# A two-layer hybrid diffusion kernel: 18 modulation chunks computed as running sums within layer 0's gates, and the x stores of layer 1 on ScalarE's queue

## The chip, the cores and the metric

One Trainium2 chip, one of its cores. The time is the device time of one execution in microseconds (us), and less is better. All data is fp32; the large products run as three fp32r matmuls over split operands.

## What is computed

Two layers over 1024 latent tokens and 256 context tokens of width 1024. In each layer a modulated RMS norm is followed by an input projection, whose columns feed three token mixers (2-D Fourier mixing, neighbourhood attention, a short gated convolution); their results are projected, gated and merged, projected again and added to x; then follows a mixture of 16 experts. What the change touches is the modulation. It comes from two condition vectors, one for the latent tokens and one for the context:

```
for l in range(DEPTH):                       # DEPTH = 2, d = 1024
    mod   = silu(c)     @ ada_w[l] + ada_b[l]   # ada_w[l]: 1024 x 6144
    mod_c = silu(c_ctx) @ ada_w[l] + ada_b[l]
    sh1, sc1, g1, sh2, sc2, g2 = split(mod, 6)  # shift, scale, gate of both halves
```

`ada_w` of both layers is 24 chunks of 512 columns, 2 MB each. For one chunk and one vector w the result is the sum over 1024 rows: 8 groups of rows (k), 128 partitions in each.

## The kernel before

The kernel is a list of stages, seven per layer (`arrive_and_project`, `conv_branch`, `fourier_branch`, `attention`, `gates_and_merge`, `mix_and_route`, `experts`) and a closing one. Each stage is a block with a program for every engine: TensorE (`pe`), ScalarE (`act`), VectorE (`dve`), GpSimd (`pool`) and SyncE (`sp`), which issues nearly all DMAs. All engines meet at the end of a stage. The order within an engine is that of the code, and the engines are held together by semaphores: `wait_ge` waits until one has a value, `then_inc` raises it when an instruction is done.

**The modulation** (class `Modulations`, lines 238 to 302). Of the 24 chunks 4 are computed at the start of layer 0. The other 20 are spread over two stages of layer 0: 16 in `conv_branch` (one after roughly every product, `ada_at`, line 861) and 4 in `fourier_branch` (`modulations`, lines 1013 and 1080). For each chunk SP loads 2 MB (line 259). `multiply` (line 273) runs 8 matmuls with the two condition columns as the stationary operand and 512 columns of weights moving, four of them side by side on strips of the array; each fp32 matmul shows as two records. VectorE copies four pairs of rows out of PSUM (line 282). After the next product `turn` (line 290) runs 4 matmuls with a 128×128 stationary operand and 2 moving columns, which transpose the rows and add the four strips. VectorE adds the bias and keeps the columns (line 298).

**The convolution** (`conv_branch`, line 840). Six work items of three products each (two halves of the channels; token spans of 512, 512 and 256), 24 fp32r matmuls per product (lines 217 to 219). VectorE multiplies, and at the end of each half runs the convolution. SP loads the cosines of the next stage when chunk 14 is multiplied (line 875).

**The Fourier stage** (`fourier_branch`, line 965). Products over the tokens with cosines and sines (line 1021), then over the channels (lines 1041 to 1057). On SP's queue stand the first chunk's load, the sines, three small tables, the other three chunk loads, each waiting for the product before it, and then the first loads of attention's q, k and bias.

**The gates** (`gates_and_merge`, line 1504). A loop over 8 groups of 128 output channels (i and b), in each over three branches (q) and three token spans of 512, 512 and 256. For each span TensorE computes the gate (24 fp32r matmuls) and the branch's projection (2, 4 and 2 fp32 matmuls for the three branches, line 1577); ScalarE takes the sigmoid (line 1595), VectorE multiplies (line 1621), and GpSimd adds branches 1 and 2 to the sum (line 1643). At a branch's first span ScalarE and VectorE round and split the next branch's gate weights (lines 1586 and 1605). SP loads the weights of the next group when a branch is through (line 1500). Three pairs of PSUM banks turn round, so TensorE may be two spans ahead of VectorE; banks 6 and 7 are free. GpSimd first clears a tile of zeros (line 1630), with which SP fills the accumulator in HBM when the last gate weights are issued.

**The start of layer 1** (`arrive_and_project`, line 326, with `layer` 1). SP loads the experts' sums for ten token tiles (line 439), the context's x, a table and weights. For each tile VectorE updates x (`update`, lines 687 and 691), ScalarE squares it (`measure`, line 585), VectorE scales and shifts (lines 699 and 707), TensorE transposes (line 485), and ScalarE (`copy_turned`, line 595) writes the rounded transposed rows over the place of x. So it waits until x is stored in HBM, by SP (line 448). SP's loop alternates between the stores of x and those of v:

```
            for t in range(NT + 2):
                if layer and t < NT:
                    sp.wait_ge(s_up, t + 1)
                    sp.dma_start(s["x_rows"][t * P:(t + 1) * P], X[:, t]).then_inc(s_xst[t % 4], 16)
                if t >= 2:
                    sp.wait_ge(s_vc, t - 1)
```

Of the kernel before, what the change touches and what calls it, by code (L numbers as in the profile page):

```python
# [231 lines left out]
def apart(eng, passed):  # L232


    eng.sem_inc(passed, 1)  # L235
# [69 lines left out]
CONV_CHUNKS = 16  # L305
FOURIER_CHUNKS = 2 * Modulations.CH - FIRST_CHUNKS - CONV_CHUNKS

# [18 lines left out]
def arrive_and_project(s, layer, last):  # L326
# [77 lines left out]
    with nc.Block() as block:  # L404
        @block.sync
        def _(sp):
# [157 lines left out]
        def _(act):  # L564
# [275 lines left out]
def conv_branch(s, layer, last):  # L840
# [16 lines left out]
    if layer == 0:  # L857
# [3 lines left out]
        ada_at = {i * 3 * len(work) // CONV_CHUNKS: i for i in range(CONV_CHUNKS)}  # L861
# [103 lines left out]
def fourier_branch(s, layer, last):  # L965
# [9 lines left out]
    ada_weights = [place(at, KD, 512)]  # L975
# [13 lines left out]
    modulate = layer == 0  # L989
    if modulate:  # L990
        ada = Modulations(s, FIRST_CHUNKS + CONV_CHUNKS, FOURIER_CHUNKS, ada_weights, place(A_ATT + 4096, 512))
    with nc.Block() as block:
        @block.sync
        def _(sp):
            s["clear_last"](sp)
            consts = s["a"]["consts"]
            if modulate:
                ada.load(sp, 0)
# [13 lines left out]
        def _(pe):  # L1012
            def modulations(i):
                if modulate and 0 < i <= FOURIER_CHUNKS:
                    ada.turn(pe, i - 1)
                if modulate and i < FOURIER_CHUNKS:
                    ada.multiply(pe, i)

# [6 lines left out]
            for w in range(2):  # L1025
                if w:
                    pe.wait_ge(s_c, 16)
                for ct in range(2):
                    over_tokens(2 * w + ct, H, ct, range(NTX), lambda m: cb[w][:, m, :])
                    modulations(2 * w + ct)  # L1030
# [12 lines left out]
            modulations(4)  # L1043
# [3 lines left out]
            if not last:  # L1047
                for w in range(2):
                    for ct in range(2):
                        over_tokens(2 * w + ct, CTX, ct, range(NTX, NT), lambda m: dctx[:, m, w, :])  # L1050
                        modulations(5 + 2 * w + ct)
# [27 lines left out]
        def _(dve):  # L1079
            def modulations(i):  # L1080
                if modulate and i:
                    ada.keep(dve, i - 1)
                if modulate and i < FOURIER_CHUNKS:
                    ada.copy(dve, i)

            if modulate:
                ada.clear_rows(dve)
# [1547 lines left out]
```

## Time and profile before

| | |
|---|---|
| median of 3 runs | 3490.39 us (3486.37 to 3490.53) |
| the profiled execution | 3491.45 us, its span 3489.7 us |
| TensorE's mean granted clock | 0.959 of full speed |
| busy, share of the span | TensorE 93%, VectorE 42%, ScalarE 26%, GpSimd 23% |
| convolution, layer 0 | about 249 to 389 us |
| Fourier stage, layer 0 | about 389 to 456 us |
| gates, layer 0 | about 631 to 1107 us |
| start of layer 1 | about 1909 us |

The profile lists every instruction of one execution, with its engine, line, start and duration. Matmuls are pipelined: records overlap, and what one costs in a row of them is the distance from start to start. An idle time in brackets stands before an instruction, with what ended it. A record's duration on TensorE doubles where the granted clock is at its lower level.

### The profile page before, as it was taken

Reading aid. Unit: us, or ns where it says so; the run is one execution under the profiler, and the core shown is the slowest. Engines: PE = TensorE matmul, PEld = TensorE weight load, DVE = VectorE, ACT = ScalarE, POOL = GpSimd, SP = SyncE. Lnnn points to the kernel's source line nnn. Section 1 sums busy time; section 2 is a strip of 40 time slices with the busy share of each in tenths; the row PEclk is TensorE's granted clock in tenths of the full one; section 3 lists DMA queues with packets and bytes.
Section 4 is the critical chain, followed back from the end, with each engine's and each line's share of the span. In section 5 each row is a group of like instructions: output and inputs, shape, how many; then the busy total and the mean of one; then the engine's idle time right before and its main releaser. Section 6 shows DMA issues by size and latency. Waiting matters only on the chain. (4 is left out here: it accounts for less than half of the span.)

```text
span 3489.7 us, 46392 instructions
## 1 busy us (share of the span) xinstructions
PE 3240.2 (93%) x16130; PEld 2425.9 (70%) x16131; DVE 1461.8 (42%) x2195; ACT 895.4 (26%) x1684; POOL 798.3 (23%) x512
## 2 busy tenths in 40 slices
PE   7999889999999969999998799899999996899996
PEld 5877568777777856667676787587777675666664
DVE  5554356211112656335351664164111156766412
ACT  4320046211112322222222321164111132222221
POOL 0230000101111234343443031000111123454342
PEclk9999989999999979999999899799999997999997
DMA  6137633111114327758685321242111333989664
GB/s 249 61 129 264 245 105 112 37 33 34 38 33 156 111 105 285 230 170 274 199 294 169 139 108 49 68 148 69 49 42 47 122 129 125 358 315 355 208 180 132
DMA packets 157104, 521.28 MB, mean 149 GB/s; under 512 B 30994, under 2 KB 81810, under 8 KB 131348
## 3 DMA queue, kind: packets, MB, share of 16 engines
q1 hardware_dynamic: 120688, 455.65, 35.1%
q0 software_dynamic: 18432, 62.96, 7.8%
q10 hardware_dynamic: 17860, 0.99, 0.4%
q8 instruction: 80, 1.31, 0.2%
q14 instruction: 44, 0.36, 0.0%
HBM read 433.00 MB, written 86.87 MB: 149 GB/s over the span
## 5 line engine op out<-in xcount | busy, mean ns | idle before, releaser
L217 PE MATMUL wide<-part,part 128*128 128x512 f32 (+2 forms) x2416 | 995.6, 412 | 67.2 <-DVE part L920 15.9
L219 PE MATMUL wide<-part,part 128*128 128x512 f32 (+2 forms) x2416 | 933.6, 386 | 0.0
L218 PE MATMUL wide<-part,part 128*128 128x512 f32 (+2 forms) x2416 | 932.4, 386 | 0.0
L217 PEld LDWEIGHTS wide<-part,part 128*128 128x128 f32 x2416 | 461.3, 191 | 197.2 <-issue 89.9
L218 PEld LDWEIGHTS wide<-part,part 128*128 128x128 f32 x2416 | 462.4, 191 | 108.0 <-issue 24.9
L219 PEld LDWEIGHTS wide<-part,part 128*128 128x128 f32 x2416 | 460.9, 191 | 93.4
L2278 PE MATMUL bank<-place,place 128*128 x864 | 379.7, 592 | 0.0
L2379 DVE CAST part<-place 128x2048 fp32r<-128x2048 f32 x128 | 183.1, 1430 | 425.8 <-DMA place<-in_w 419.2
L2381 DVE TENSOR_TENSOR part<-place,part 128x2048 fp32r<-128x2048 f32 x128 | 321.5, 2512 | 4.4
L2278 PEld LDWEIGHTS bank<-place,place 128*128 128x128 f32 x864 | 159.9, 190 | 180.8 <-issue 180.8
L1643 POOL TENSOR_TENSOR place<-place,place 128x512 f32 (+1 forms) x80 | 111.5, 1394 | 742.8 <-DVE place L1621 742.8
L1621 DVE TENSOR_TENSOR place<-wide,place 128x512 f32<-128x512 f32 (+1 forms) x80 | 55.4, 692 | 516.8 <-PE wide L1577 476.5
L2411 POOL TENSOR_TENSOR part<-place,part 128x512 fp32r<-128x512 f32 x116 | 189.9, 1649 | 195.3 <-ACT part L2318 195.3
L217 PE MATMUL bank<-part,part 128*128 128x512 f32 (+1 forms) x576 | 218.9, 380 | 0.0
L219 PE MATMUL bank<-part,part 128*128 128x512 f32 (+1 forms) x576 | 202.2, 351 | 0.0
L218 PE MATMUL bank<-part,part 128*128 128x512 f32 (+1 forms) x576 | 202.0, 351 | 0.0
L1577 PE MATMUL wide<-place,place 128*128 128x512 f32 x416 | 191.4, 591 | 0.0
L1595 ACT ACTIVATE place<-wide 128x512 f32<-128x512 f32 x80 | 47.8, 597 | 484.6 <-PE wide L219 484.5
L2432 POOL DMA_INDIRECT acc<-place,toadd x58 | 123.3, 2125 | 191.3 <-ACT place L2356 179.2
L2356 ACT ACTIVATE place<-bank,toadd 128x512 f32<-128x512 f32 x108 | 74.3, 688 | 272.4 <-PE bank L2278 263.1
L1388 DVE CUSTOM_DVE_ANT_0 place<-wide,place 128x640 f32<-128x640 f32 (+1 forms) x144 | 111.7, 775 | 51.6 <-PE wide L1298 51.4
L819 POOL TENSOR_TENSOR place<-place,place 128x512 f32<-128x512 f32 x34 | 51.4, 1511 | 346.3 <-DVE place L791 346.3
(247 smaller groups left out, 3824.9 us busy)
## 6 DMA issues: line engine op xcount, KB each, us to landing
place<-in_w SPq DMA_DIRECT2D x124, 1024.0 KB, 15.1
place<-in_w SPq DMA_DIRECT2D x34, 2048.0 KB, 9.6
place<-in_ada_w SPq DMA_DIRECT2D x24, 2048.0 KB, 9.3
place<-in_w_gates SPq DMA_DIRECT2D x32, 640.0 KB, 4.1
place<-in_bias SPq DMA_DIRECT2D x96, 192.0 KB, 3.6
x_rows<-place SPq DMA_DIRECT2D x28, 512.0 KB, 2.9
place<-in_w_rows SPq DMA_DIRECT2D x6, 2048.0 KB, 7.6
place<-in_w_gates SPq DMA_DIRECT2D x16, 768.0 KB
```

Of the source, the lines that this page charges most:

```text
L217: pe.matmul(out, left[0], right[0], start=first, stop=False)
L218: pe.matmul(out, left[0], right[1], start=False, stop=False)
L219: return pe.matmul(out, left[1], right[0], start=False, stop=last)
L1388: dve.tensor_tensor_reduce(out=pr[n % 2][h][:, 0:w], in0=wide[h][:, 0:w], in1=to_add, scale=1.0, scalar=-3e38, op0=ALU.add, op1=ALU.max, a ...
L1577: mm = pe.matmul(banks[2 * (n % 3) + 1][:, 0:tn], wb[q][:, KD + k, :], src[:, k, t0:t0 + tn], start=k == 0, stop=k == ks - 1)
L1643: pool.tensor_tensor(to, to, prod[c % 2][:, 0:tn], ALU.add).then_inc(s_mg, 1)
L2278: mm = pe.matmul(banks[6 + h][:], gt[:, k, :], w2[:, bass.ds(slots[b], 1), k, h * 512:(h + 1) * 512] .rearrange("p o n -> p (o n)"), start ...
L2356: act.activation(yb[b][:, h * 512:(h + 1) * 512], banks[6 + h][:], ACT.Copy, scale=weight[b])\
L2379: dve.tensor_copy(whi[:, b, at], w13[:, b, at]).then_inc(s_whi, 1)
L2381: dve.tensor_tensor(wlo[:, b, at], w13[:, b, at], whi[:, b, at].bitcast(F32), ALU.subtract)\
L2411: pool.tensor_tensor(xlo[b][:, at], xraw[b][:, at], xhi[b][:, at].bitcast(F32), ALU.subtract)\
L2432: pool.indirect_dma_start(out=s["acc"], out_offset=bass.IndirectOffsetOnAxis(toadd[b][:, 0:1], 0), in_=yb[b], in_offset=None, compute_op=A ...
```

## The change

The convolution keeps 2 of its 16 chunks, the Fourier stage none of its 4. The other 18 move into the gates of layer 0, three into each of the first six of its eight channel groups, one per branch. There a chunk comes in four pieces of 512 KB (two groups of rows each) over two buffers, issued by ScalarE on its own queue. VectorE multiplies each group of rows by its condition value per partition and adds it to a running sum, one for each condition: 16 operations on 128×512 per chunk, pieces 0 and 1 ahead of the first span's gating, pieces 2 and 3 ahead of the second's. TensorE then only adds over the partitions, behind the third span: 8 matmuls with 128×128 of a sum as the stationary operand and one column of ones moving. The sums stand in bank 6, and VectorE adds the bias. The last two channel groups are outside the loop on all engines, since their place in the arena holds the pieces, and GpSimd clears its zeros after the sixth group. In layer 1 the x stores are issued by ScalarE in `measure`, ahead of the square, and SP's loop holds only the v stores.

```diff
@@ -302,8 +302,8 @@
 
 
 FIRST_CHUNKS = 4
-CONV_CHUNKS = 16
-FOURIER_CHUNKS = 2 * Modulations.CH - FIRST_CHUNKS - CONV_CHUNKS
+CONV_CHUNKS = 2
+GATE_CHUNKS = 2 * Modulations.CH - FIRST_CHUNKS - CONV_CHUNKS
 
 
 def norm_row(s, v, w):
@@ -442,13 +442,9 @@
                             sp.dma_start(X[:, q], s["x_rows"][q * P:(q + 1) * P]).then_inc(s_x[q], 16)
                 sp.dma_start(trig, s["a"]["trig"]).then_inc(s_trig, 16)
                 load_weights(sp, Q)
-            for t in range(NT + 2):
-                if layer and t < NT:
-                    sp.wait_ge(s_up, t + 1)
-                    sp.dma_start(s["x_rows"][t * P:(t + 1) * P], X[:, t]).then_inc(s_xst[t % 4], 16)
-                if t >= 2:
-                    sp.wait_ge(s_vc, t - 1)
-                    sp.dma_start(s["v_rows"][(t - 2) * P:(t - 1) * P], res[(t - 2) % 4]).then_inc(s_st[(t - 2) % 4], 16)
+            for t in range(NT):
+                sp.wait_ge(s_vc, t + 1)
+                sp.dma_start(s["v_rows"][t * P:(t + 1) * P], res[t % 4]).then_inc(s_st[t % 4], 16)
             sp.wait_ge(s_mm, N1)
             load_weights(sp, K)
             for m, (c, t) in enumerate(second):
@@ -576,6 +572,7 @@
             def measure(t):
                 if layer:
                     act.wait_ge(s_up, t + 1)
+                    act.dma_start(s["x_rows"][t * P:(t + 1) * P], X[:, t]).then_inc(s_xst[t % 4], 16)
                     to = XN[:, t]
                 else:
                     act.wait_ge(s_x[t], 16)
@@ -858,7 +855,7 @@
...
-        ada_at = {i * 3 * len(work) // CONV_CHUNKS: i for i in range(CONV_CHUNKS)}
+        ada_at = {2 + i * 3 * len(work) // CONV_CHUNKS: i for i in range(CONV_CHUNKS)}
     segs = [(0, SEQ, 0)] + ([] if last else [(SEQ, CTX, SEQ + 2)])
     s_ahead = sem("cosines_loaded")
     s_whi, s_wlo, s_mm, s_zero = sem("weights_hi"), sem("weights_lo"), sem("conv_product"), sem("conv_zeros")
@@ -986,36 +982,22 @@
...
-    modulate = layer == 0
-    if modulate:
-        ada = Modulations(s, FIRST_CHUNKS + CONV_CHUNKS, FOURIER_CHUNKS, ada_weights, place(A_ATT + 4096, 512))
...
-            if modulate:
-                ada.load(sp, 0)
...
-            if modulate:
-                for i in range(1, FOURIER_CHUNKS):
-                    ada.load(sp, i)
             load_queries_and_keys(s, sp, 0, last, s_qk, s_qk)
             load_bias_rows(s, sp, layer, 0, 0, s_qk)
             sp.wait_ge(s_qk, 16 * NL)
...
@@ -1524,16 +1488,33 @@
...
+    ada = layer == 0
+    pieces = [place(A_R + 6 * TOK + b * D, 2, 512) for b in range(2)]
+    sums = place(at + 2048, 2, 512)
+    ones = place(at + 2048 + D, 8)
+    ada_w = s["a"]["ada_w"].rearrange("l c p k n -> (l c) p k n")
+    mods = s["mod"][:].rearrange("p l c w -> p (l c) w")
+    if ada:
+        s_pl = [sem(f"ada_w_loaded_{b}") for b in range(2)]
+        s_ac, s_sum, s_keep, s_one = sem("ada_sums"), sem("mod_columns"), sem("mod_kept"), sem("ones")
     U = 3 * NS
     work = [(q, span) for q in range(3) for span in range(NS)]
 
-    def chunks(eng, body):
+    def first_ada(i, b, q):
+        return i * 3 + (3 * b + q + FIRST_CHUNKS + CONV_CHUNKS)
+
+    def ada_steps(i, b, q, n):
+        return i * 48 + (48 * b + 16 * q + n + 1)
+
+    def chunks(eng, body, between=None):
 
         with eng.Fori(0, KD - 3, 2) as i:
             for b in range(2):
-                body(i, b, False)
+                body(i, b, False, ada)
+        if between is not None:
+            between()
         for b in range(2):
-            body(KD - 2, b, b == 1)
+            body(KD - 2, b, b == 1, False)
 
     with nc.Block() as block:
         @block.sync
@@ -1559,24 +1540,35 @@
         @block.tensor
         def _(pe):
             pe.sem_inc(s_bm, U)
...
+
+            def body(i, b, final, modulate):
...
+                    if modulate and span == 2:
+                        pe.wait_ge(s_ac, ada_steps(i, b, q, 16))
+                        for j in range(4):
+                            for w in range(2):
+                                mm = pe.matmul(banks[6][:, 2 * j + w:2 * j + w + 1], sums[:, w, j * P:(j + 1) * P],
+                                               ones[:, 0:1], start=True, stop=True)
+                        mm.then_inc(s_sum, 1)
+
+            if ada:
+                pe.wait_ge(s_one, 1)
+            chunks(pe, body)
...
@@ -1585,14 +1577,29 @@
...
-            def body(i, b, final):
+            def load_piece(i, b, q, p):
+                act.wait_ge(s_ac, ada_steps(i, b, q, max(4 * p - 4, 0)))
+                act.dma_start(pieces[p % 2], ada_w[bass.ds(first_ada(i, b, q), 1), :, 2 * p:2 * p + 2]
+                              .rearrange("o p k n -> p (o k) n")).then_inc(s_pl[p % 2], 16)
+
+            def body(i, b, final, modulate):
...
+                    if modulate and n == 0 and b == 0:
+                        load_piece(i, b, q, 0)
...
                     act.activation(sg[m % 2][:, 0:tn], banks[2 * (n % 3)][:, 0:tn], ACT.Sigmoid).then_inc(s_sg, 1)
+                    if modulate and span == 0:
+                        load_piece(i, b, q, 2)
+                        load_piece(i, b, q, 3)
+                    if modulate and span == 1 and (b, q) != (1, 2):
+                        for p in range(2):
+                            act.wait_ge(s_ac, ada_steps(i, b, q, 12 + 4 * p))
+                            load_piece(i, b + (q + 1) // 3, (q + 1) % 3, p)
...
@@ -1604,11 +1611,33 @@
...
-            def body(i, b, final):
+            def add_piece(i, b, q, p):
+                dve.wait_ge(s_pl[p % 2], i * 96 + (96 * b + 32 * q + 16 * (p // 2) + 16))
+                for kk in range(2):
+                    for w in range(2):
+                        n = 4 * p + 2 * kk + w
+                        col = s["silu"][:, 2 * p + kk, w:w + 1]
+                        if n >= 2:
+                            dve.wait_ge(s_ac, ada_steps(i, b, q, n - 1))
+                            dve.scalar_tensor_tensor(sums[:, w], pieces[p % 2][:, kk], col, sums[:, w], ALU.mult, ALU.add)\
+                                .then_inc(s_ac, 1)
+                        else:
+                            dve.tensor_scalar(sums[:, w], pieces[p % 2][:, kk], col, None, ALU.mult).then_inc(s_ac, 1)
+
+            def keep_mods(i, b, q):
+                dve.wait_ge(s_sum, i * 3 + (3 * b + q + 1))
+                dve.tensor_tensor(mods[:, bass.ds(first_ada(i, b, q) * 4, 4)], banks[6][:, 0:8].rearrange("p (t w) -> p t w", w=2),
+                                  s["vec"][:, bass.ds(first_ada(i, b, q) * 4 + V_ADAB, 4)].unsqueeze(2)
+                                  .broadcast_to([P, 4, 2]), ALU.add).then_inc(s_keep, 1)
+
+            def body(i, b, final, modulate):
                 for n, (q, span) in enumerate(work):
                     (t0, tn), m = spans[span], b * U + n
                     if span == 0 and not (final and q == 2):
                         leave_weights(i + (b + (q + 1) // 3), (q + 1) % 3)
+                    if modulate and span < 2:
+                        add_piece(i, b, q, 2 * span)
+                        add_piece(i, b, q, 2 * span + 1)
...
@@ -1620,27 +1649,39 @@
...
+                    if modulate and span == 2:
+                        keep_mods(i, b, q)
 
             dve.sem_inc(s_pr, 3)
+            if ada:
+                dve.sem_inc(s_ac, 1)
+                dve.memset(ones, 1.0).then_inc(s_one, 1)
             leave_weights(0, 0)
             chunks(dve, body)
+            if ada:
+                dve.wait_ge(s_keep, GATE_CHUNKS)
 
         @block.gpsimd
         def _(pool):
-            pool.memset(zeros, 0.0).then_inc(s_zero, 1)
+            def clear():
+                if ada:
+                    pool.wait_ge(s_sum, GATE_CHUNKS)
+                pool.memset(zeros, 0.0).then_inc(s_zero, 1)
+
+            def body(i, b, final, modulate):
...
+
             pool.sem_inc(s_mg, 2)
...
+            chunks(pool, body, clear)
...
```

The other hunks take `modulations` out of the Fourier stage on TensorE and VectorE, and put the loop bodies of TensorE and GpSimd in the gates into a function `body`, unchanged but for what is shown.

## Rows read from the trace of the kernel before

**Rows 1.** Layer 0's gates: busy TensorE, weight loads, VectorE, ScalarE, GpSimd; clock, DMA share, GB/s.

```profile
750.00:800.00 50.00, 50.00 (x232) 38.49 (x231) 8.00 (x11) 9.65 (x13) 6.00 (x5) 1.00 0.14 42
```

**Rows 2.** TensorE in the convolution: start, us, engine, line, operation, shapes, count, [idle].

```profile
265.97 0.95 PE L290 MATMUL bank<-select,place 128*128 128x2 f32 x8
266.85 1.90 PE L273 MATMUL bank<-place,silu 128*2 128x512 f32 x16
268.68 0.50 PE L217 MATMUL wide<-part,part 128*128 128x512 f32 x1
269.01 0.39 PE L218 MATMUL wide<-part,part 128*128 128x512 f32 x1
269.24 0.40 PE L219 MATMUL wide<-part,part 128*128 128x512 f32 x1
```

**Rows 3.** TensorE in the Fourier stage.

```profile
406.72 0.95 PE L290 MATMUL bank<-select,place 128*128 128x2 f32 x8
409.37 3.50 PE L273 MATMUL bank<-place,silu 128*2 128x512 f32 x16 [1.70 <-DMA place<-in_ada_w]
412.81 7.18 PE L1021 MATMUL wide<-place,place 128*128 128x512 f32 x16
...
432.31 3.73 PE L1021 MATMUL wide<-place,place 128*128 128x1 f32 x32
435.90 2.87 PE L1041 MATMUL bank<-place,place 128*128 128x512 f32 x4
...
444.79 1.71 PE L290 MATMUL bank<-select,place 128*128 128x2 f32 x8
447.07 0.59 PE L1046 MATMUL bank<-place,place 128*128 128x2 f32 x2 [0.58 <-DVE place L1095]
```

**Rows 4.** The start of layer 1: ScalarE, SP's issue of the x stores, and TensorE's first transposition.

```profile
1916.17 1.06 ACT L585 ACTIVATE place<-place 128x1024 f32<-128x1024 f32 x1 [11.27 <-DVE place L691]
1937.42 1.08 ACT L595 ACTIVATE part<-bank 128x512 fp32r<-128x512 f32 x2 [15.57 <-DMA x_rows<-place]
1922.98 19.09 SPq L448 DMA_DIRECT2D x_rows<-place  x3
1921.76 1.97 PE L485 MATMUL bank<-ident,place 128*128 128x128 f32 x8 [6.37 <-DVE place L707]
```

**Rows 5.** VectorE in layer 0's gates, the third spans of branches 2, 0 and 1.

```profile
753.41 0.42 DVE L1621 TENSOR_TENSOR place<-bank,place 128x256 f32<-128x256 f32 x1 [3.04 <-PE bank L1577]
...
771.55 0.42 DVE L1621 TENSOR_TENSOR place<-bank,place 128x256 f32 x1 [3.04 <-PE bank L1577]
772.02 1.23 DVE L1605 TENSOR_TENSOR part<-place,part 128x1024 fp32r<-128x1024 f32 x1
...
793.93 0.42 DVE L1621 TENSOR_TENSOR place<-bank,place 128x256 f32<-128x256 f32 x1 [3.91 <-PE bank L1577]
```

**Rows 6.** VectorE's nearest operations in shape, in the convolution and in layer 1.

```profile
382.99 2.60 DVE L955 SCALAR_TENSOR_TENSOR place<-place,vec,place 128x1024 f32<-128x1024 f32 x2
387.28 1.00 DVE L955 SCALAR_TENSOR_TENSOR place<-place,vec,place 128x256 f32<-128x256 f32 x2
2023.42 0.42 DVE L771 TENSOR_SCALAR place<-place 128x512 f32<-128x512 f32 x1
```

**Rows 7.** DMA issues: line, count, KB each, us to landing; in the gates, then the page.

```profile
place<-in_w_gates SPq DMA_DIRECT2D x14, 640.0 KB, 4.0
place<-in_dft SPq DMA_DIRECT2D x4, 2048.0 KB, 9.2
```

**Rows 8.** Two lines' instructions, duration ns min/median/max: VectorE beside GpSimd, GpSimd's additions.

```profile
L1931 DVE TENSOR_TENSOR part<-place,part x32: 676/687/2860, 1108.9 to 2816.0; 128x512 fp32r<-128x512 f32 x32
L1643 POOL TENSOR_TENSOR place<-place,place x80: 721/1294/2022, 664.2 to 2788.2; 128x512 f32 x64, 128x256 f32 x16
```

**Rows 9.** Landing of the loads of line 439 and of the x stores of line 448.

```profile
DMA to landing us min/median/max: 4.3/7.7/9.3
...
DMA to landing us min/median/max: 2.6/2.9/14.5
```

More of the change, by code:

```diff
@@ L1079, in _ @@
         def _(dve):
[L1080 to L1087, printed above, removed]
-            for i in range(4):
-                modulations(i)
             for ct in range(2):
@@ L1100, in _ @@
             if not last:
-                for i in range(5, FOURIER_CHUNKS + 1):
-                    modulations(i)
                 for ct in range(2):
@@ L1561, in _ @@
             pe.sem_inc(s_bm, U)
-            with pe.Fori(0, KD - 1, 2) as i:
-                for b in range(2):
-                    for n, (q, span) in enumerate(work):
-                        t0, tn = spans[span]
-                        src, ks = branches[q]
-                        if span == 0:
-                            pe.wait_ge(s_w[q], i * 16 + (b * 16 + 16))
-                            pe.wait_ge(s_whi, i * 3 + (b * 3 + q + 1))
-                            pe.wait_ge(s_wlo, i * 3 + (b * 3 + q + 1))
-                        pe.wait_ge(s_pr, i * U + (b * U + n + 1))
-                        for k in range(KD):
-                            mm = split_product(pe, by_tile(banks[2 * (n % 3)][:, 0:tn]), (whi[q][:, k, :], wlo[q][:, k, :]),
-                                               (tiles_of(HI, k, t0, tn), tiles_of(LO, k, t0, tn)), k == 0, k == KD - 1)
-                        mm.then_inc(s_gm, 1)
-                        for k in range(ks):
-                            mm = pe.matmul(banks[2 * (n % 3) + 1][:, 0:tn], wb[q][:, KD + k, :], src[:, k, t0:t0 + tn],
-                                           start=k == 0, stop=k == ks - 1)
-                        mm.then_inc(s_bm, 1)
@@ new lines, in body @@
+            def body(i, b, final, modulate):
+                for n, (q, span) in enumerate(work):
+                    t0, tn = spans[span]
+                    src, ks = branches[q]
+                    if span == 0:
+                        pe.wait_ge(s_w[q], i * 16 + (b * 16 + 16))
+                        pe.wait_ge(s_whi, i * 3 + (b * 3 + q + 1))
+                        pe.wait_ge(s_wlo, i * 3 + (b * 3 + q + 1))
+                    pe.wait_ge(s_pr, i * U + (b * U + n + 1))
+                    for k in range(KD):
+                        mm = split_product(pe, by_tile(banks[2 * (n % 3)][:, 0:tn]), (whi[q][:, k, :], wlo[q][:, k, :]),
+                                           (tiles_of(HI, k, t0, tn), tiles_of(LO, k, t0, tn)), k == 0, k == KD - 1)
+                    mm.then_inc(s_gm, 1)
+                    for k in range(ks):
+                        mm = pe.matmul(banks[2 * (n % 3) + 1][:, 0:tn], wb[q][:, KD + k, :], src[:, k, t0:t0 + tn],
+                                       start=k == 0, stop=k == ks - 1)
+                    mm.then_inc(s_bm, 1)
+                    if modulate and span == 2:
[5 more added lines that the diff above has]
+                        mm.then_inc(s_sum, 1)
```

35 lines of the change are left out of this document (11 added, 24 removed).

## The prediction

> **What bounds the kernel now.** I first read the busy time by stretch: in the stage of layer 0's gates TensorE is busy for every microsecond, at the full granted clock, while VectorE works 8.0 of 50 us, ScalarE 9.7 and GpSimd 6.0, with the DMA engines 14% busy [rows 1]. So whatever is added to TensorE there is added to the time one for one, and what is given to the others is free as long as it arrives in time. Then TensorE's timeline in the convolution: a modulation chunk is two pieces between two gate-free products, the multiplication (16 records, 268.68 − 266.85 = 1.83 us) and the turn (8 records, 266.85 − 265.97 = 0.88 us), and TensorE goes on without a hole [rows 2]. The same pieces stand in the Fourier stage, with one real wait for a weight load [rows 3]. Last, the start of layer 1: ScalarE waits until 1937.42 for the store of the first x tile, which SP issued at 1922.98, though the tile was ready when ScalarE squared it at 1916.17; TensorE had transposed it by 1923.7 [rows 4].
>
> **Removed from the convolution.** 14 multiplications go: 14 × 1.83 = 25.6 us. Of the 16 turns the last lies behind the last product, under VectorE's closing work; 15 are on TensorE's path before and 2 after: 13 × 0.88 = 11.4. The first product after a multiplication has one step of 0.33 instead of 0.23 us (268.68 to 269.01 against 269.01 to 269.24): 14 × 0.10 = 1.4. Together **−38.5**. No new wait comes up: the start waits for VectorE's split as before, the end for VectorE's convolution as before, and the cosines now load behind chunk 0, far earlier. The 14 loads of 2 MB leave SP's queue, where nobody waited for them. VectorE's 56 copies of rows and 14 additions were beside TensorE: nothing.
>
> **Removed from the Fourier stage.** The slots of four chunks [rows 3]: the first multiplication, 1.83 as in rows 2; 406.72 to 412.81, 6.09 (turn, a wait for the load, and a multiplication at the lower clock); and two pairs as in rows 2, 2.71 each. The last turn at 444.79 ran before a wait that ended at 447.07 anyway: nothing. Sum **−13.3**. The sines' load, 2 MB landing in 9.2 us [rows 7], is then covered by the two products over the cosines, 7.2 us each as at 412.81; and q, k and bias loads, queued behind the chunk loads on SP, are issued some 25 us earlier, so SP's closing wait isn't late.
>
> **Added to TensorE in the gates.** Per chunk 8 matmuls with a 128×128 fp32 stationary operand and one column, that is 16 records. The nearest row is exactly this shape: 32 records from 432.31 to 435.90 [rows 3], 0.112 us each, so 16 are 1.80; with one slow first step 1.90. From the turn's two-column rows [rows 2] it is 2 × 0.88 = 1.76; from a half-clock turn (444.79, 8 records in 1.71 [rows 3]) 3.42 at the worst. I take the full clock because TensorE doesn't rest here: 18 × 1.90 = **+34.2** (bounds 1.76, and 2.1 with two more slow steps: 31.7 to 37.8).
>
> **Does the chunk arrive in time?** With T = 0 where TensorE starts a branch q, a branch takes 18.1 us from one third span to the next for branches 0 and 2 and 22.4 for branch 1 [rows 5], which the spans share by their widths of 512, 512 and 256: 7.2, 7.2 and 3.6. The first gate is through at T + 5.5 (24 matmuls of 0.23 [rows 2]). The sums stand behind the third span, at T + 18.0 (22.3). VectorE first splits the next weights (1.23 us, done at T + 1.6, as 772.02 + 1.23 lies 1.7 behind 771.55). Its pieces: `tensor_scalar` on 512 elements is 0.42 us; for `scalar_tensor_tensor` there are 1.30 us for 1024 elements and 0.50 for 256, so 0.77 for 512 (dependent operations, 0.04 between them; here each waits for the last but one, so this is the upper end, and 0.53, the slope of 1.04 ns alone, the lower) [rows 6]. Pieces 0 and 1 are then done by T + 1.6 + 0.9 + 6 × 0.8 = 7.3, and the gating multiplication waits about 0.2 us: TensorE has two work items of slack in PSUM, so nobody notices. ScalarE issues piece 2 after its sigmoid, at T + 6.2 + 0.4; a load of 640 KB lands in 4.0 us in this stage [rows 7], so 512 KB is there at T + 10.5. Eight operations of 0.8 bring it to T + 16.9, against 18.0. VectorE holds 16 operations, 11.9 us, and 3.3 us of its old work in a period of 19.9: 76%. ScalarE, which now waits on those sums before it issues, has only the third span's sigmoid (T + 17.2) queued behind the issue at about T + 17: under a microsecond, covered by the same slack. The piece loads, 2 MB in 20 us beside SP's gate weights, raise the DMA share to about half (0.14 goes with 42 GB/s [rows 1]). So I cost all this at nothing, with 1.1 us of cover per chunk of branches 0 and 2, and 5.4 in branch 1. If the cover goes, each late microsecond costs TensorE one. Keeping the modulation, the later clearing of zeros on GpSimd (the 11 MB fill is issued only behind the last gate weights) and TensorE's unrolled last two chunks: nothing, at most 1 us each way.
>
> **GpSimd beside VectorE.** The new operations read two SBUF tensors while GpSimd's additions do the same. A VectorE operation with two SBUF inputs takes 0.69 us alone and up to 2.86 us beside GpSimd, whose additions take 0.7 to 1.3 and up to 2.0 [rows 8]. In a branch 1 or 2 there are three additions; at most one (0.7 to 1.3 us) falls into the stretch that counts, since VectorE waits for its piece or for TensorE when the others run. The Trainium skill, page "SBUF — State Buffer", section "Who interferes with whom", makes this an exclusive lock held for a whole instruction, whoever starts first. By that rule the sum could grow by about 5 us (rival 1).
>
> **The x stores.** ScalarE issues the first at 1916.2 (0.4 us, ahead of the square and so on the path). Unloaded, such a store lands in 2.9 us; the loads in this saturated stretch took up to 9.3; the store queued behind them 14.5 [rows 9]. The copy needs TensorE's transposition at 1923.7, moved to 1924.1. I take some 7 us as a load here does: landed at 1923.7, the copy starts at 1924.3 instead of 1937.4, 13.1 gained; the second tile's store, issued at about 1926 and needed at 1932.5, may give back 1: **−12.0** (5 to 13). Behind it TensorE runs without waits, so the shift carries through. Ten issues of 0.4 us on ScalarE are beside TensorE's work; the v stores on SP get one wait fewer.
> The Trainium skill, page "DMA: Bandwidth & Descriptors", section "Issuing engines are not separate DMA queues", speaks against this part: DMAs of all issuers run on the same 16 engines, and several issuers save issue time only. If that were all, these 12 us would stay away and the sum would be −17.6; rival 2 works the mechanism out.
>
> **Sum.** −38.5 − 13.3 + 34.2 − 12.0 = **−29.6 us**. The durations come from an execution of 3491.45 us (span 3489.7 and 1.75 around it), 1 us above the median of the three runs, 3490.39. The forecast is 3490.4 − 29.6 = **3460.8 us**. A measurement of this kernel can tell about 0.2%, 7 us.
>
> **Rivals.**
> 1. *VectorE's chain ends after TensorE's third span.* For: only 1.1 us of cover; GpSimd's additions. Against: the upper price is used already. With two additions (2.6 us) in the way it is 0.9 late in six chunks of branch 2, about 5 us: 3466.
> 2. *The x store still lands late.* If it takes 14.5 us from 1916.6, the copy starts at 1931.1, and the gain is 6.3 instead of 12: 3466. If it waits for everything queued around it and lands when it did, the gain is 0: 3473. For: 2.9 us unloaded, 14.5 here [rows 9]. Against: it would have to wait for loads that SP issues after it.
> 3. *The sums run at the half clock* (3.42 us a chunk): +27, 3488, no change. It needs TensorE to stop before them; the rows show a lower clock only after such stops.
> 4. *The piece loads are late, and it is slower than before.* Place: piece 2 is issued only after the sigmoid, at T + 6.6, and eight operations (6.4) follow. TensorE waits from a landing time of 5.0 us on, in the 12 chunks of branches 0 and 2; the gain of 29.6 is gone at 5.0 + 29.6 / 12 = 7.5 us. At the 9.3 us of the saturated stretch [rows 9] it is 4.3 × 12 = 52: 3512. Against: 4.0 us for more bytes in this very stage [rows 7].
>
> **Chances.** The forecast as it stands 0.72, rival 1 0.10, rival 2 0.08, rival 3 0.03, rival 4 0.05, nothing of these (an unseen gap at TensorE's new loop exit, no net change) 0.02. So faster by over 0.2% 0.90, within 0.2% 0.05, slower 0.05. The range: downwards the low ends of the sums (31.7) and the high end of the store (13), and the 4 us by which the runs differ, 3453; upwards rivals 1 and 2 together (5 and 6) with 37.8 for the sums (4), 3476.
>
> **What the changed profile would show.** The convolution some 38 us shorter, with two groups of 16 records of the multiplication; the Fourier stage 13 us shorter; layer 0's gates 34 us longer with TensorE still busy throughout, 18 groups of 16 records of about 1.9 us and no idle time before them; 288 VectorE operations of 0.4 to 0.8 us, piece loads of about 4 us; and in layer 1 the first copy of transposed tiles about 13 us sooner. I am wrong if TensorE waits for VectorE ahead of the sums, if the groups take over 2.1 us, or if ScalarE still waits 10 us for the x store.

## The result, and the profile after

The changed kernel takes **3457.94 us** (median of 4 runs, 3452.30 to 3458.65), the kernel before beside it 3490.46 (4 runs, 3486.37 to 3491.18): a ratio of 0.9906, 95% interval 0.9889 to 0.9923, so 32.5 us less where 29.6 were forecast. Taken again later (e8_changed_again below), the ratio was 0.9903.

Below, each stage by the start of TensorE's first record in the next one. These are durations between two such marks, in one profiled execution of each kernel:

| stretch | before, us | after, us | change | forecast |
|---|---|---|---|---|
| convolution of layer 0 (250.32 / 249.72 to Fourier) | 139.03 | 99.17 | −39.9 | −38.5 |
| Fourier stage | 67.07 | 55.67 | −11.4 | −13.3 |
| attention | 177.07 | 176.65 | −0.4 | 0 |
| gates | 473.76 | 505.75 | +32.0 | +34.2 |
| mix | 192.90 | 195.78 | +2.9 | 0 |
| experts | 608.21 | 608.51 | +0.3 | 0 |
| start of layer 1, to the first product | 31.12 | 16.79 | −14.3 | −12.0 |
| layer 1 from there to its last mark | 1523.09 | 1521.90 | −1.2 | 0 |

The busy time of the whole execution, from the page (busy us, share of the span, instructions):

```profile
span 3456.9 us, 46809 instructions
PE 3222.9 (93%) x15986; PEld 2438.2 (71%) x15987; DVE 1599.0 (46%) x2411; ACT 895.5 (26%) x1684; POOL 789.7 (23%) x512
```

VectorE carries 137 us more than before (1461.8 there), and TensorE never waits for what was added. Layer 0's gates by stretch (us, busy TensorE, weight loads, VectorE, ScalarE, GpSimd; granted clock, DMA share, GB/s), the whole stage:

```profile
581.20:1086.90 505.70, 503.79 (x2400) 391.63 (x2400) 261.96 (x401) 66.50 (x101) 57.60 (x49) 0.99 0.37 122
```

and the same stage in the kernel before:

```profile
633.50:1107.20 473.70, 471.74 (x2112) 359.33 (x2112) 70.94 (x95) 66.41 (x100) 62.04 (x48) 1.00 0.15 50
```

TensorE is idle for about 2 us of this stretch in both; its one wait of the stage in the trace after, 3.5 us for VectorE's first split, ends where the stretch begins. VectorE's work grew by 191 us, and the stage by 32.0, all of it TensorE's own records. The clock of 0.99 is a low stretch at the stage's start, which the kernel before has too; from 600 us on it is 1.00. Here is one chunk of branch 2 on VectorE (start, us, engine, line, operation, shapes, count, [idle before, and what ended it]):

```profile
756.05 0.17 DVE L1629 TENSOR_TENSOR mod<-bank,vec 128x8 f32 x1 [1.40 <-PE bank L1565]
756.19 1.23 DVE L1612 TENSOR_TENSOR part<-place,part 128x1024 fp32r<-128x1024 f32 x1
757.33 0.88 DVE L1625 TENSOR_SCALAR place<-place,silu 128x512 f32<-128x512 f32 x2
758.12 4.06 DVE L1622 SCALAR_TENSOR_TENSOR place<-place,silu,place 128x512 f32<-128x512 f32 x6
763.21 0.69 DVE L1650 TENSOR_TENSOR place<-wide,place 128x512 f32<-128x512 f32 x1 [1.03 <-PE wide L1558]
765.72 5.39 DVE L1622 SCALAR_TENSOR_TENSOR place<-place,silu,place 128x512 f32<-128x512 f32 x8 [1.81 <-DMA place<-in_ada_w]
```

and TensorE's adding of the chunk before it, followed by the first product of this branch:

```profile
753.93 1.84 PE L1565 MATMUL bank<-place,place 128*128 128x1 f32 x16
755.64 0.47 PE L217 MATMUL wide<-part,part 128*128 128x512 f32 x1
```

With T = 755.64, the second half of the sums starts at T + 10.1 when piece 2 lands (10.5 forecast) and ends at 765.72 + 5.39 = 771.11, T + 15.5 (16.9 forecast). TensorE adds this chunk at 773.86, so the cover is 2.75 us; over all 18 chunks it is 2.4 to 2.8 in the 12 of branches 0 and 2 and 5.9 to 6.1 in the 6 of branch 1. VectorE waits for landing pieces 17 times, 22.4 us in all, and never passes that on to TensorE. A lone line of instructions with minimum, median and maximum duration in ns shows the new operations on VectorE, GpSimd's additions beside them, the page then the pieces' landing (count, KB each, us):

```profile
L1622 DVE SCALAR_TENSOR_TENSOR place<-place,silu,place x252: 733/745/1783, 586.5 to 962.5; 128x512 f32<-128x512 f32 x126
L1681 POOL TENSOR_TENSOR place<-place,place x80: 721/1294/2076, 613.9 to 2756.4; 128x512 f32 x48, 128x512 f32<-128x512 f32 x16, 128x256 f32 x12, 128x256 f32<-128x256 f32 x4
```

```profile
place<-in_ada_w ACTq DMA_DIRECT2D x72, 512.0 KB, 4.3
```

At layer 1's start, ScalarE issues the store itself and TensorE's first product no longer waits for 15.76 us. Before, it was:

```profile
1939.48 0.55 PE L217 MATMUL wide<-part,part 128*128 128x256 f32 x1 [15.76 <-DVE part L715]
```

After, ScalarE and then TensorE:

```profile
1898.35 0.38 ACTq L575 DMA_DIRECT2D x_rows<-place  x1
1898.77 1.06 ACT L582 ACTIVATE place<-place 128x1024 f32<-128x1024 f32 x1 [11.05 <-DVE place L688]
...
1905.87 1.09 ACT L592 ACTIVATE part<-bank 128x512 fp32r<-128x512 f32 x2 [1.42 <-DMA x_rows<-place]
```

```profile
1904.36 1.97 PE L481 MATMUL bank<-ident,place 128*128 128x128 f32 x8 [4.74 <-DVE place L704]
1908.04 0.55 PE L217 MATMUL wide<-part,part 128*128 128x256 f32 x1 [1.71 <-DVE part L712]
```

From issue to copy are 7.5 us, the 7 of the forecast; what is left of ScalarE's wait for the store is 1.42 us. (The first product's wait is put down to VectorE's split, which works on ScalarE's copy and so stands behind the store.)

### The profile page after: what moved, and what is told of

Same layout as the page of the kernel before. It is cut to its first block and busy times, and to the rows that moved or that the text cites. A ratio compares the mean times of both kernels' runs of the same rounds, so it can differ in the third digit from the quotient of the medians.

```text
span 3456.9 us, 46809 instructions
## 1 busy us (share of the span) xinstructions
PE 3222.9 (93%) x15986; PEld 2438.2 (71%) x15987; DVE 1599.0 (46%) x2411; ACT 895.5 (26%) x1684; POOL 789.7 (23%) x512
## 5 line engine op out<-in xcount | busy, mean ns | idle before, releaser
L217 PE MATMUL wide<-part,part 128*128 128x512 f32 (+2 forms) x2416 | 992.2, 411 | 54.2 <-DVE part L917 15.9
L1681 POOL TENSOR_TENSOR place<-place,place 128x512 f32 (+3 forms) x80 | 106.3, 1329 | 1107.0 <-DVE place L1650 1107.0
L2422 DVE TENSOR_TENSOR part<-place,part 128x2048 fp32r<-128x2048 f32 x128 | 314.5, 2457 | 4.4
L1622 DVE SCALAR_TENSOR_TENSOR place<-place,silu,place 128x512 f32<-128x512 f32 x252 | 176.6, 769 | 22.6 <-DMA place<-in_ada_w 22.4
## 6 DMA issues: line engine op xcount, KB each, us to landing
place<-in_ada_w SPq DMA_DIRECT2D x6, 2048.0 KB, 16.9
```

The source lines that it names most:

```text
L217: pe.matmul(out, left[0], right[0], start=first, stop=False)
L1622: dve.scalar_tensor_tensor(sums[:, w], pieces[p % 2][:, kk], col, sums[:, w], ALU.mult, ALU.add)\
L1681: pool.tensor_tensor(to, to, prod[c % 2][:, 0:tn], ALU.add).then_inc(s_mg, 1)
L2422: dve.tensor_tensor(wlo[:, b, at], w13[:, b, at], whi[:, b, at].bitcast(F32), ALU.subtract)\
```

## Experiments

**The store alone** (e1_stores_alone): the kernel before, with this only.

```diff
@@ SP, projections
-            for t in range(NT + 2):
-                if layer and t < NT:
-                    sp.wait_ge(s_up, t + 1)
-                    sp.dma_start(s["x_rows"][t * P:(t + 1) * P], X[:, t]).then_inc(s_xst[t % 4], 16)
...
@@ ScalarE, measure(t)
                     act.wait_ge(s_up, t + 1)
+                    act.dma_start(s["x_rows"][t * P:(t + 1) * P], X[:, t]).then_inc(s_xst[t % 4], 16)
```

> Only the second part: the x stores of layer 1 on ScalarE's queue, all 20 chunks where they were. My theory: the two parts don't touch each other, and this one gives what the traces show for it, the first product of layer 1 some 14 us sooner, so 3490.5 - 14 = 3476.5 us. Rival: the interleaving with SP's loads only happens to go well beside the other part; then under 8 us. Rival (queues on the same engines save issue time only): 0 to 1 us.

Measured: 3476.19 us (6 runs) against 3490.02, ratio 0.9961 (0.9948 to 0.9973), −13.8 us. TensorE's first product of layer 1 waits 1.72 us where it had waited 15.76, and ScalarE's copy now waits for TensorE, not for the store. That is the forecast, and both rivals (under 8 us, 0 to 1 us) fall:

```profile
1926.39 0.60 ACT L592 ACTIVATE part<-bank 128x512 fp32r<-128x512 f32 x1 [1.12 <-PE bank L481]
```

**The sums alone** (e2_sums_alone): the changed kernel with those lines back on SP.

> Only the first part: the sums in the gates, with the x stores on SP's queue as before. My theory: 39.9 (convolution) and 11.4 (Fourier stage) come off, 32.0 is added in the gates, so -19.3: 3471.2 us. The stage of mixing and routing in layer 0 was 2.9 us longer in the changed kernel's profile: if the change causes that, it is there again and the time is 3474; if it comes and goes with the clock, it isn't there in every profile.

Measured: 3466.09 us (5 runs), ratio 0.9929 (0.9916 to 0.9942), −23.9 us. The gates take 505.68 us, as in the whole change, and the wait at layer 1's start is back (13.46 us ahead of the first product). The gain is 4.6 us more than the 19.3 expected, just outside its interval (20.2 to 29.3). The expectation was added up from one profile's stages, and the Fourier stage, 55.67 us in it, moves by some us between executions (e8 below). The mix takes 195.88 us, as in the whole change. The two parts give −37.7 together and the whole gave −32.5; the intervals of the parts are ±4.5 us each and that of the whole ±6, so the difference isn't shown to be one.

**The store ahead on SP's own queue** (e5_store_ahead_on_sp): the kernel before, in which SP issues the first store right behind the `acc` loads, ahead of the trigonometric rows and Q's weights. It stays on SP's queue, so it parts two things that the change moves together: the engine that issues, and the place among the loads.

```diff
+                sp.wait_ge(s_up, 1)
+                sp.dma_start(s["x_rows"][0:P], X[:, 0]).then_inc(s_xst[0], 16)
                 sp.dma_start(trig, s["a"]["trig"]).then_inc(s_trig, 16)
...
-                if layer and t < NT:
+                if layer and 0 < t < NT:
```

> The kernel before, with one thing moved: SP issues the store of x tile 0 right behind the ten loads of the experts' sums, ahead of the rotation table and of 2 MB of weights. My theory: what made the store late was its place in SP's queue, so most of the gain of ScalarE's queue comes without it: issued near 1922, landed in 6 to 8 us, a gain of 7 to 9 us, 3482 us. Rival (the queue itself counts, ScalarE's has the engines' turns for itself): the store still lands with SP's backlog after 12 us or more, and the gain is under 4 us, 3487 us.

Measured: 3485.84 us (10 runs), ratio 0.9989 (0.9979 to 0.9998), −4.2 us. SP's timeline, then ScalarE's:

```profile
1916.21 9.84 SPq L439 DMA_DIRECT2D place<-acc  x6
1926.09 0.43 SPq L444 DMA_DIRECT2D x_rows<-place  x1
```

```profile
1919.36 1.06 ACT L587 ACTIVATE place<-place 128x1024 f32<-128x1024 f32 x1 [11.27 <-DVE place L693]
1933.36 1.09 ACT L597 ACTIVATE part<-bank 128x512 fp32r<-128x512 f32 x2 [8.31 <-DMA x_rows<-place]
```

From the square to the copy are 14.0 us here, 21.3 before [rows 4] and 7.1 after. The copy comes 7.3 us after the issue, where it had taken 14.4: that half is the store's place behind the trigonometric rows and Q's weights, and it doesn't need ScalarE. The rest is issue time: SP is busy until 1926.05 with the `acc` issues, while the tile was ready at 1919.36. In the profile the first product's wait fell from 15.76 to 8.50, 7.3 us; the runs' −4.2 (interval −7.3 to −0.7) holds this only at its end, and by the runs alone the rival's "under 4 us" isn't excluded. What speaks against the rival is the store's own time, 7.3 us where it wanted 12 or more. One thing stays untested: in the changed kernel SP issues Q's weights at 1906.15, when ScalarE's copy has already begun (1905.87), so no run shows how a store on ScalarE's queue fares when it is issued behind them.

**The adding twice** (e3_adding_twice): the changed kernel, with the same eight matmuls of a chunk run a second time. It only repeats work.

```diff
-                        for j in range(4):
+                        for j in (0, 1, 2, 3) * 2:
```

> The changed kernel with each chunk's 8 matmuls over the partitions run twice. My theory: TensorE has no slack in the gates and a row of 16 records costs 1.8 us: 18 x 1.8 = +32, 3490 us. Rival: VectorE's chain or the gating sets the period of a branch, and the matmuls lie in its shadow: +0 to +10, under 3468 us.

Measured: 3518.49 us (4 runs), ratio 1.0076 (1.0061 to 1.0091), so 60.6 us over the changed kernel and not 32. The theory's 32 is right for the records and wrong for the time, and the rival (under 3468) falls. The stage is 561.81 us long, 56.1 more; where the other 4.5 of the median lie isn't shown. No new wait: TensorE's only one is still the 3.5 us at the start. A group of 32 records takes 3.63 us where 16 took 1.84, which gives 18 × 1.79 = 32.2. The other 24 us are clock. The columns are those of the stage's line above, with the granted clock third from the end:

```profile
582.60:1144.40 561.80, 559.85 (x2688) 440.81 (x2689) 261.87 (x401) 66.43 (x101) 57.70 (x49) 0.95 0.33 109
600.00:640.00 40.00, 40.00 (x203) 32.31 (x202) 21.05 (x34) 3.85 (x6) 3.62 (x3) 0.91 0.36 116
700.00:720.00 20.00, 20.00 (x101) 16.65 (x101) 9.00 (x15) 1.92 (x3) 3.15 (x3) 0.91 0.37 124
720.00:740.00 20.00, 20.00 (x103) 16.13 (x103) 11.41 (x19) 5.20 (x6) 2.01 (x2) 0.91 0.32 102
760.00:780.00 20.00, 20.00 (x101) 14.93 (x99) 8.24 (x11) 2.52 (x4) 3.74 (x3) 1.00 0.41 122
```

TensorE is busy for 20.00 of 20 us and gets 0.91 on average, that is, part of the stretch at the lower of its two levels, 1.2 GHz. No stop came before it; what came before was a long group of one-column records. In the 20 us from each group's start the clock is 0.91 for 15 of the 18 groups and 1.00 for the other three, so the group makes the fall likely and not certain.

**A second set with 128 columns** (e7_second_adding_wide): as before, but the second set multiplies by the identity, 128 columns, into another bank. It too only adds work that no one reads.

```diff
+                        for j in range(4):
+                            for w in range(2):
+                                mm = pe.matmul(banks[7][:, j * P:(j + 1) * P], sums[:, w, j * P:(j + 1) * P],
+                                               s["ident"][:], start=True, stop=True)
```

> Adding twice cost 60.6 us, not 32: its trace shows the granted clock at 0.91 in most windows of 20 us of the gates, with no idle time on TensorE. Here the second adding of each chunk has 128 moving columns instead of 1: the same 16 weight loads, nearly the same time of a record (0.117 us against 0.112), more columns. My theory: the clock falls after long groups of records with one column, since the array does little in them; with wide ones it stays up, and only the records themselves cost: 18 x 1.9 = +34, 3492 us. Rival: any longer group of fp32 matmuls with a new weight load each takes the clock down: 3518 us again.

Measured: 3490.94 us (10 runs), ratio 0.9999 (0.9987 to 1.0011): 34 over the changed kernel beside it (e8_changed_again). The stage grew by 32.2 us, the records' own time, and its clock is full:

```profile
581.30:1119.30 538.00, 536.01 (x2688) 423.62 (x2689) 261.88 (x401) 66.50 (x102) 57.66 (x49) 1.00 0.34 114
600.00:640.00 40.00, 40.00 (x208) 31.73 (x207) 21.59 (x33) 4.45 (x7) 3.91 (x4) 1.00 0.40 125
700.00:720.00 20.00, 20.00 (x104) 16.01 (x102) 13.27 (x21) 1.86 (x4) 2.83 (x3) 1.00 0.24 75
```

The same number of records, the same stage and the same VectorE work; what differs is the second set's columns, and the bank that it writes. So the 24 us of the run before come with the doubled one-column records, and neither with the number of matmuls nor with VectorE. The bank was not tried alone; the one-column groups themselves were no slower for it (3.63 us for 32, twice 1.84 less the overlap). Whether their standing 32 in a row decides, or their number in the stage, was not parted either, though each of the 15 falls comes within 5 us of a group's start.

**VectorE longer** (e4_vector_longer): the changed kernel, with a reduction of 4096 elements that no one reads, 4.42 us, between pieces 2 and 3 of every chunk. This takes the cover away.

```diff
+                        if span == 1:
+                            dve.tensor_reduce(more, HI[:, 0:4].rearrange("p t k n -> p (t k n)").bitcast(F32), AX.X, ALU.add).then_inc(s_more, 1)
```

> The changed kernel with one more VectorE operation per chunk, a sum over 4096 elements between pieces 2 and 3 (about 4.4 us by the price per element of the others). In the changed kernel's trace the running sums end 2.4 to 2.9 us before TensorE adds them in 12 chunks and about 6 us in the 6 of branch 1. My theory: that is all the cover there is; 12 chunks come 1.8 us late, +22 us, 3480 us, and TensorE waits ahead of the adding. Rival: VectorE's time is free beside TensorE as long as its busy share stays under 1 (it would be near 0.85 here): 3458 us.

Measured: 3490.70 us (10 runs), ratio 1.0006 (0.9997 to 1.0016), 34 over the changed kernel beside it and not 22; the rival (3458) falls. TensorE's waits in the stage (us in all, times, longest):

```profile
PE bank L1566 <- DVE place L1623: 17.3, 12, 1.8
PE wide L217 <- DVE part L1613: 3.5, 1, 3.5
```

Twelve chunks are late by 1.1 to 1.8 us, none of them in branch 1: 4.42 less a cover of 2.4 to 2.8 is 1.6 to 2.0. The stage grew by 37.0, more than twice the 17.3 of the waits. The granted clock fell behind several of them, where a wait and the one-column group stood together (the second group at 2.89 us instead of 1.84; windows with the columns as above):

```profile
647.25 1.95 PE L1566 MATMUL bank<-place,place 128*128 128x1 f32 x16 [1.67 <-DVE place L1623]
670.25 2.89 PE L1566 MATMUL bank<-place,place 128*128 128x1 f32 x16 [1.24 <-DVE place L1623]
```

```profile
640.00:660.00 20.00, 18.33 (x86) 14.19 (x85) 15.57 (x19) 2.52 (x4) 2.00 (x2) 0.91 0.37 112
660.00:680.00 20.00, 18.76 (x85) 15.32 (x84) 15.14 (x19) 1.92 (x3) 0.00 (x0) 0.83 0.37 112
```

So less than 2 us of lateness in twelve chunks already cost the whole gain: the "one for one" of the prediction is too kind.

**Rows by a one-hot operand** (e6_rows_by_one_hot): a better form of the adding. The sums are now the moving operand, in quarters of 256 columns, and the stationary one is a 128×32 window of zeros with a single column of ones, which puts chunk r's sum into row r of a bank. Six chunks gather there; then VectorE copies the rows, TensorE turns them (2 transpositions) and VectorE adds the bias.

```diff
                         for j in range(4):
-                            for w in range(2):
-                                mm = pe.matmul(banks[6][:, 2 * j + w:2 * j + w + 1], sums[:, w, j * P:(j + 1) * P],
-                                               ones[:, 0:1], start=True, stop=True)
+                            mm = pe.matmul(banks[6][32 * j:32 * j + 32, 0:256], one_hot[:, 31 - r:63 - r],
+                                           sums[:, j // 2, j % 2 * 256:j % 2 * 256 + 256], start=r == 0, stop=r == 5)
...
+                        if r == 5:
+                            for h in range(2):
+                                pe.wait_ge(s_row, i + (h + 1))
+                                pe.transpose(banks[7][:, h * P:(h + 1) * P], rows[:, h * P:(h + 1) * P], s["ident"][:])\
+                                    .then_inc(s_turn, 1)
```

> A version meant to beat both: the sums are the moving operand, in four quarters of 256 columns on four strips of the array at once, and the stationary operand is 32 columns of zeros with ones in the column of the chunk, so that six chunks add up into rows of one bank; after six chunks VectorE copies it, TensorE transposes two blocks, and VectorE adds the bias to 24 columns with four small operations. My theory: the cost per chunk falls from 1.84 us to about 0.55 (four strips side by side, as the old multiplication's rows show), 18 x 1.3 = -23, and three transpositions with a wait of 1 to 2 us give back up to 8: 3443 us. Rival: the four quarters run one after the other, 1.7 us: nothing is gained, and 3 to 8 us are lost, 3464 us.

Measured: **3446.07 us** (4 runs, 3439.72 to 3449.39), ratio 0.9877 (0.9861 to 0.9894), 10.5 us less than the changed kernel beside it and faster than both. The stage is 491.49 us long, 14.3 less. One chunk's group, and the waits of the stage:

```profile
745.77 0.64 PE L1567 MATMUL bank<-place,place 128*32 128x256 f32 x8
```

```profile
PE wide L217 <- DVE part L1619: 3.5, 1, 3.5
PE bank L1573 <- DVE place L1639: 1.2, 3, 0.4
```

18 × (1.84 − 0.64) = 21.6; the three turnings give back 21.6 − 14.3 = 7.3 us, of which 1.2 are waits for the copies. The theory (3443) held and the rival (3464) fell. Two things changed at once, the operands' roles and the four quarters of the output side by side, and they were not parted.

**The changed kernel again** (e8_changed_again), beside the last three on their chip.

> The changed kernel itself beside the others, on the same chip. It should be 0.991 of the kernel before, some 3458 us. In its first profile the clock showed two dips of 0.83 over 10 us in layer 0's mixing and routing, where the kernel before has none. If they belong to the changed order they are there again, if they are chance they are elsewhere or gone.

Measured: 3456.59 us (4 runs, 3450.54 to 3459.14) against 3490.15, ratio 0.9903 (0.9884 to 0.9923). The gates take 505.73 us, as before. The rest of layer 0 is not the same in this second profile of the same kernel: the Fourier stage takes 51.19 us instead of 55.67 and the mix 194.06 instead of 195.78, with one stretch at 0.91 and TensorE busy instead of two, and at another place. So a single profile's time of these two stages is good to some us only.

## Why the prediction was right, point by point

The forecast was 3460.8 and the measurement 3457.9, 2.9 us off. The mechanism was right: work leaves two stages, comes back cheaper in a third, and a wait goes. That the total is so close is partly luck: the misses are of 1 to 3 us each and of both signs, and two of the stages move by as much between executions of the same kernel (e8).

- **TensorE bounds the gates, the others are free there: shown.** VectorE took on 191 us there, and TensorE's idle time didn't change; 32.2 us more of TensorE's records (e7) lengthened the stage by 32.2.
- **Convolution, −38.5:** it was −39.9, from the same two kinds of groups (−40.9 in e8's profile).
- **Fourier stage, −13.3:** it was −11.4 in this profile and −15.9 in e8's, of the same kernel. Behind the 32 one-column records of `over_tokens` the next group takes 3.76 us here, and the granted clock of the 10 us around it is 0.58; the kernel before has 2.87 [rows 3] and 0.84 (430 to 440 us). In e8 it is 1.96:

```profile
348.89 34.77 PE L1003 MATMUL wide<-place,place 128*128 128x512 f32 x96 [7.72 <-PEq L864]
383.52 3.76 PE L1022 MATMUL bank<-place,place 128*128 128x512 f32 x4
```

```profile
380.00:390.00 10.00, 7.92 (x30) 5.17 (x30) 1.29 (x2) 0.94 (x3) 0.00 (x0) 0.58 0.00 0
```

```profile
385.06 1.96 PE L1022 MATMUL bank<-place,place 128*128 128x512 f32 x4
```

  The removed multiplication stood right ahead of those records [rows 3], but its going doesn't explain the lower clock: it is gone in all seven profiles with the sums in the gates, and the group takes 3.76 us in the changed kernel, e2 and e7 and 1.96 in e3, e4, e6 and e8. The stage takes 51.2 to 57.2 us in these seven, and 67.1 to 69.3 in the three without the sums. So the forecast lies within what the term moves by, 3 us to either side of it; what decides whether the clock falls there stays open.
- **Adding, +34.2 (18 × 1.90):** it was +32.0. A group takes 1.84 us in the profile, the next product starts 1.71 us behind the group's start (753.93 to 755.64), and 32.0 / 18 is 1.78. The slow first step that I added hardly shows, and the nearest row in shape (1.80 for 16) was the better price.
- **The chunk in time: shown, with cover to spare.** I gave 1.1 and 5.4 us, it was 2.4 to 2.8 and 5.9 to 6.1. What was mis-sized is the 0.8 us per operation: eight in a row, each of which needs the last but one, took 5.39, 0.67 each, since one starts before the end of the one before it (745 ns each). Rival 4 (late pieces) needed a landing of 5.0 us; it was 4.3. The run e4 shows that a late chunk does hold TensorE up, as rivals 1 and 4 have it, and that one for one was set too low: 17.3 us of waits made 37.0 of stage.
- **GpSimd beside VectorE (rival 1):** six of the 252 `scalar_tensor_tensor` took 1777 to 1783 ns instead of 745, each started while one of GpSimd's additions was running, and the six beside which an addition started later took 750 to 754. This agrees with the Trainium skill's page "SBUF — State Buffer", section "Who interferes with whom", by which the later of the two waits for the earlier; but no chunk of the 18 came within 2 us of TensorE's adding.
- **The x store, −12.0:** it was −14.3 from the start of the transition to the first product and −13.8 ± 4.4 alone. The landing was as forecast; the 1 us that the second store might give back wasn't given back. Rival 2 fell. The Trainium skill's page "DMA: Bandwidth & Descriptors" ("Issuing engines are not separate DMA queues") gives a second issuer nothing but issue time. By the profile that is 6.9 us of it (14.0 to 7.1 from square to copy, e5 against after); the other 7.3 came from the store's not standing behind the trigonometric rows and Q's weights, which e5 got on SP's own queue. So the rule isn't contradicted, but it is no reason to expect nothing: issue time was half of what was gained, and the place among the loads the other half.
- **Rival 3 (sums at the half clock)** didn't come about, but the reason that I gave against it, "the rows show a lower clock only after such stops", is wrong as e3 shows: 32 one-column records in a row brought the clock down, behind 15 of 18 groups, with TensorE busy throughout. With 16, the gates of the changed kernel stayed at full clock in both profiles. So the rival was nearer than the 0.03 that I gave it: doubling the group was enough.
- **Not foreseen: +2.9 us in the mix** (+1.2 in e8's profile). Two stretches of the mix run at 0.91 with TensorE busy, where the kernel before has 1.00:

```profile
1160.00:1180.00 20.00, 20.00 (x104) 17.05 (x104) 12.13 (x14) 6.71 (x11) 9.57 (x6) 0.91 0.24 84
1220.00:1240.00 20.00, 20.00 (x97) 16.82 (x97) 12.34 (x25) 6.37 (x10) 6.62 (x5) 0.91 0.26 103
```

  They are there in the changed kernel, in e2, e3, e6 and e7, once in e8, and not in e1, e4 and e5. So they are seen only with the sums, in six of seven profiles, and the store alone doesn't bring them; the stage's own code is the same. e6 has no one-column records in the gates and shows them too, so those aren't the cause. It stays open.

## What to carry to other kernels

Work may be moved off a bound engine even where it costs the other engine several times as much (191 us of VectorE for the 51 us of TensorE that left the two stages before, 32 of which came back), as long as its end is dated against the moment at which the bound engine asks for it, chunk by chunk. Leave that cover a margin (here 1.1 to 1.8 us of lateness in twelve chunks used up a gain of 34), because a late arrival can cost more than its own length when the clock falls behind it. Before a term of a few us is called exact, look at a second profile of the same kernel. And when a small transfer is late, look at two things apart: when its issuer gets to it, and what is ahead of it on its queue. For a sum over partitions, the form with the data as the moving operand, 256 columns wide, in four quarters side by side, took 0.64 us here where the one-column form took 1.84; it is worth trying first.

## What the hardware showed that I had not expected

- A group of 32 records with one moving column (3.63 us) lowered TensorE's granted clock to 0.91 over the 20 us from its start, behind 15 of 18 groups and with no idle time at all, 24 us in sum; 16 of them (1.84 us) didn't, and 16 with 128 columns behind those 16 didn't either.
- The same code in two executions, or in two kernels that differ elsewhere, ran its Fourier stage in 51.2 to 57.2 us, by where the granted clock stood low.
- `scalar_tensor_tensor` operations of 128x512 elements, each of which needs the result of the last but one, follow each other every 0.67 us though each lasts 745 ns.
- Four matmuls of fp32 with a 128×32 stationary operand and 256 columns each, aimed at four different quarters of the output partitions, took 0.64 us together as 8 records whose median is 390 ns each, so they overlap; eight 128×128 ones with one column took 1.84.
